# Retention scores of two heads in one step, and a new plan of who sums which modulation block

## What is computed

```python
mod = c_act @ w_ada[l] + b_ada[l]
shift, scale, gate = jnp.split(mod, 3, axis=-1)
h = _rmsnorm(x, norm_g[l]) * (1.0 + scale[:, None, :]) + shift[:, None, :]
z = h @ w_in[l]                      # 13 pieces of 512 columns
# Fourier mix, neighbourhood attention, retention, convolution, each times silu(gate piece)
y = jnp.concatenate([o_fft, o_na, o_ret, o_cv], axis=-1) @ w_out[l]
x = x + gate[:, None, :] * y
```

## Time and profile before

| | us |
|---|---|
| median of 3 runs | 2259.01 |
| lowest and highest of them | 2250.01, 2264.5 |
| the profiled execution | 2253.18 |
| its span | 2251.6 |
| TensorE busy in the span | 2164.1 (96%) |
| VectorE busy | 1480.2 (66%) |
| ScalarE busy | 962.4 (43%) |
| moved by DMA | 509.82 MB, mean 226 GB/s |

### The profile page before, as it was taken

The page is one execution under the profiler, slowest core; times in us unless marked ns, Lnnn a source line. Parts: engine busy times, 40 slices in busy tenths (PEclk is TensorE's granted clock), DMA queues, the critical chain, the costliest instruction groups (busy, mean ns, idle before and its releaser), DMA issues.

```text
span 2251.6 us, 33030 instructions
## 1 busy us (share of the span) xinstructions
PE 2164.1 (96%) x13686; PEld 1808.6 (80%) x13686; DVE 1480.2 (66%) x1904; ACT 962.4 (43%) x1337; POOL 201.7 (9%) x385
## 2 busy tenths in 40 slices
PE   5979999999899999999999999999999999999998
PEld 3768878887878878886888888787777989988876
DVE  0445879876655887765696756667776868445654
ACT  2324554554434554555632222223446444444443
POOL 2201111110011111100010100000100001000000
PEclk8989999999999999999999999999999999999999
DMA  9989886777598777676485646454875778422253
GB/s 367 401 265 311 275 319 234 273 269 275 153 315 299 258 265 250 226 269 235 157 294 162 219 131 196 152 184 147 284 256 174 238 249 280 136 67 65 88 188 131
DMA packets 225454, 509.82 MB, mean 226 GB/s; under 512 B 36065, under 2 KB 40289, under 8 KB 222753
## 3 DMA queue, kind: packets, MB, share of 16 engines
q1 hardware_dynamic: 170320, 300.49, 39.9%
q0 software_dynamic: 54304, 202.79, 26.3%
q10 hardware_dynamic: 688, 4.55, 0.5%
HBM read 499.38 MB, written 8.39 MB: 226 GB/s over the span
## 4 chain that ended last, share of the span: by engine, by line
PE 79%; DMA 8%; DVE 7%; ACT 2%; issue 2%; SPq 1%; POOL 0%; DVEq 0%; ACTq 0%; POOLq 0%
PE ps L768 23%; PE ps L769 22%; PE ps L770 22%; PE ps L824 3%; DMA w_raw<-in_w_in 3%; DMA ada_raw<-in_ada_w 2%; DVE ada_acc L2172 2%; PE ps L1439 1%; DVE wl L2252 1%; DMA rsw<-in_ada_w 1%; SPq L604 1%; DMA w_raw<-in_w_out 1%; PE ps L956 1%; PE ps L969 1%; PE ps L1165 1%
## 5 line engine op out<-in xcount | busy, mean ns | idle before, releaser
L2259 DVE TENSOR_TENSOR wl<-w_raw,wh 128x1024 fp32r<-128x1024 f32 x280 | 334.8, 1222 | 243.7 <-ACT wh L1543 242.6
L1543 ACT ACTIVATE wh<-w_raw 128x1024 fp32r<-128x1024 f32 x280 | 291.7, 1056 | 384.6 <-PE ps L770 253.6
L1596 ACT ACTIVATE wh<-w_raw 128x1024 fp32r<-128x1024 f32 x220 | 230.7, 1058 | 435.1 <-PE ps L770 391.0
L768 PE MATMUL ps<-hh,wh 128*128 128x256 f32 x1280 | 374.4, 292 | 11.2 <-DVE hl L2312 8.1
L2252 DVE TENSOR_TENSOR wl<-w_raw,wh 128x1024 fp32r<-128x1024 f32 x220 | 266.7, 1221 | 178.6 <-ACT wh L1596 178.4
L769 PE MATMUL ps<-hh,wl 128*128 128x256 f32 x1280 | 362.5, 283 | 0.0
L770 PE MATMUL ps<-hl,wh 128*128 128x256 f32 x1280 | 361.9, 283 | 0.0
L2172 DVE SCALAR_TENSOR_TENSOR ada_acc<-ada_raw,cpad,ada_acc 128x1024 f32<-128x1024 f32 x264 | 330.8, 1280 | 15.4 <-DMA ada_raw<-in_ada_w 13.2
L768 PEld LDWEIGHTS ps<-hh,wh 128*128 128x128 f32 x1280 | 244.2, 191 | 37.0 <-issue 21.5
L768 PE MATMUL ps<-wh,act_hl 128*128 128x512 f32 x640 | 256.6, 401 | 0.2 <-DVE wl L2252 0.2
L769 PE MATMUL ps<-wh,act_hl 128*128 128x512 f32 x640 | 253.3, 396 | 0.0
(11 more groups left out here) (374 smaller groups left out, 3346.1 us busy)
## 6 DMA issues: line engine op xcount, KB each, us to landing
ada_raw<-in_ada_w POOLq DMA_DIRECT2D x272, 512.0 KB, 5.1
w_raw<-in_w_in SPq DMA_DIRECT2D x208, 512.0 KB, 5.6
w_raw<-in_pool_in SPq DMA_DIRECT2D x72, 512.0 KB, 4.6
w_raw<-in_w_out SPq DMA_DIRECT2D x64, 512.0 KB, 5.6
w_raw<-in_mla_in SPq DMA_DIRECT2D x56, 512.0 KB, 4.6
ada_fourth<-in_ada_w POOLq DMA_DIRECT2D x48, 512.0 KB, 6.0
w_raw<-in_pool_out SPq DMA_DIRECT2D x48, 512.0 KB, 5.0
w_raw<-in_mla_out SPq DMA_DIRECT2D x32, 512.0 KB, 4.2
```

The source lines that it names most:

```text
L768: pe.matmul(dst, ah, bh, start=start, stop=False, skip_group_check=True)
L1543: act.activation(wh[:, g % RING, :], w_raw[:, g % RING, :], ACT.Copy).then_inc(w_hi, 1)
L1596: act.activation(wh[:, r, :], w_raw[:, r, :], ACT.Copy).then_inc(w_hi, 1)
L2259: dve.tensor_tensor(wl[:, g % RING, :], w_raw[:, g % RING, :], wh[:, g % RING, :].bitcast(F32), ALU.subtract).then_inc(w_lo, 1)
```

## The change

1. **Scores.** At every second step from 16 to 22, TensorE multiplies heads h and h + 1 together: four instructions, alternately on rows 0 to 63 and 64 to 127, head h into bank 4, head h + 1 into bank 5. It waits for `rt_p` of head h - 1, as before. VectorE reads bank `4 + h % 2`. Bank 5 is thus in use from step 16 to 23.
2. **Plan.** No modulation block is summed on TensorE in steps 17 to 24. Blocks by step (layer 0, VectorE + TensorE): steps 3 to 6 had 10 in all and now have 16, steps 8 to 11 had 14 and now have 11, step 18 had 2 + 0 and steps 19 to 24 had 2 + 2 each (now 1 + 0, at step 24 2 + 0), steps 27 to 31 had 1, 0, 2, 1, 1 and now have 4, 5, 3, 3, 3. Layer 1: steps 3 to 8 are as before; steps 10, 12 and 14 to 17 have one more each, on VectorE; steps 18 to 24 had 1 + 3, 1 + 3, then 1 + 2 (2 + 2 at 24) and now have 1, 1, 0, 0, 0, 0, 0; steps 25 to 32 had 0, 3, 3, 2, 2, 3, 3, 0 and now have 4, 4, 4, 4, 5, 1, 5, 5.
3. **The last piece is shared.** Of piece 5, VectorE sums the first 8 blocks in layer 0 and the first 10 in layer 1, TensorE the others; `ada_sum` then adds VectorE's part onto the same bank. In layer 1 this piece is for two conditioning vectors, so each of VectorE's 10 blocks takes two instructions, and the sum two vectors. In all TensorE sums 94 blocks where it summed 112, in 57 groups where there were 67 (counted from the tables by the rule of `ada_middle`); VectorE runs 28 instructions more; the sums over partitions are of 8 vectors, where they were of 5.
4. The first sum at step 24 waits for the last `rt_p` (which step 24 waits for in any case), piece 3 of layer 0 is summed in bank 6, and the context's first turn waits for `small_mul` instead of a read of bank 4.

```diff
--- before.py
+++ after.py
@@ -88,26 +88,51 @@
 TAP_ORDER = [CENTRE] + [i for i in range(TAPS) if i != CENTRE]
 
 
-def spread(j, t0, counts):
-
-    k, out = 0, {}
+def spread(j, t0, counts, k=0, end=ADA_SLOTS):
+
+    out = {}
     for t, n in enumerate(counts):
         out[t0 + t] = [(j, k + i) for i in range(n)]
         k += n
-    assert k == ADA_SLOTS
+    assert k == end
     return out
 
 
-ADA_DVE = [{**spread(0, 0, [1] * 8 + [2, 1, 2, 1, 2]), **spread(1, 13, [1, 2, 1] + [2] * 6),
-            **spread(3, 22, [2] * 5 + [1, 0, 2, 1, 1, 1])},
-           {**spread(0, 0, [1] * 2 + [2] * 5 + [1, 2, 1]), **spread(1, 10, [1] * 14 + [2])}]
-ADA_PE = [{**spread(2, 3, [1, 1, 2, 2, 2, 2, 3, 3]), **spread(4, 12, [4] + [3] * 4), **spread(5, 19, [2] * 8)},
-          {**spread(2, 2, [1, 2, 2, 2, 3, 3, 3]), **spread(3, 11, [3] * 4 + [2] * 2), **spread(4, 18, [3] * 2 + [2] * 5),
-           **spread(5, 26, [3, 3, 2, 2, 3, 3])}]
-ADA_FIN = [{11: 2, 17: 4, 18: 0, 27: 5, 28: 1, 34: 3}, {9: 2, 10: 0, 17: 3, 25: 4, 28: 1, 32: 5}]
-ADA_SUMMED = [(0, 1, 3), (0, 1)]
+def joined(*parts):
+
+    out = {}
+    for part in parts:
+        for t, slots in part.items():
+            out.setdefault(t, []).extend(slots)
+    return out
+
+
+ADA_SPLIT = [8, 10]
+ADA_DVE = [joined(spread(0, 0, [1, 1, 1, 2, 2, 2, 2, 1, 2, 1, 1]),
+                  spread(1, 11, [1, 2, 1, 2, 2, 2, 2, 1, 1, 1, 1]),
+                  spread(3, 22, [1, 1, 2, 2, 1, 1, 2, 2, 2, 2]),
+                  spread(5, 26, [1] * 8, 0, ADA_SPLIT[0])),
+           joined(spread(0, 0, [1] * 2 + [2] * 5 + [1, 2, 1]),
+                  spread(1, 10, [2, 1, 2, 1, 2, 2, 2, 2, 1, 1]),
+                  spread(5, 25, [1] * 6 + [2] * 2, 0, ADA_SPLIT[1]))]
+ADA_PE = [joined(spread(2, 3, [2, 2, 2, 2, 2, 3, 3]), spread(4, 12, [4] + [3] * 4),
+                 spread(5, 25, [2] * 4, ADA_SPLIT[0])),
+          joined(spread(2, 2, [1, 2, 2, 2, 3, 3, 3]), spread(3, 11, [3] * 4 + [2] * 2),
+                 spread(4, 25, [3, 3, 3, 3, 4]), spread(5, 31, [3, 3], ADA_SPLIT[1]))]
+ADA_FIN = [{10: 2, 11: 0, 17: 4, 24: 1, 32: 3, 34: 5}, {9: 2, 10: 0, 17: 3, 24: 1, 30: 4, 33: 5}]
+ADA_SUMMED = [(0, 1, 3, 5), (0, 1, 5)]
 ADA_BANKS = [7 if t <= 17 else 5 for t in range(STEPS)]
-ADA_FIN_BANKS = [ADA_BANKS, [4 if t == 28 else b for t, b in enumerate(ADA_BANKS)]]
+ADA_FIN_BANKS = [[6 if t == 32 else b for t, b in enumerate(ADA_BANKS)], ADA_BANKS]
+
+
+def ada_vectors(l, j):
+
+    return ((0, 1), (1, 2)) if l + (j > 1) == DEPTH else ((ADA_SUMMED[l].index(j) % 2, 0),)
+
+
+def ada_begins(l, j):
+
+    return ADA_SPLIT[l] if j == 5 else 0
 ADA_AHEAD = range(8, SMALL_STEP)
 CTX_SSQ, CTX_VAR = OUT_STEP + 2, OUT_STEP + 4
 CTX_TURN = {(5, 0): 0, (5, 1): 1, (5, 3): 2, (6, 0): 3, (6, 2): 4, (6, 3): 5, (7, 1): 6, (7, 2): 7}
@@ -214,7 +239,7 @@
 
 ADA_MORE, DVE_AFTER = ada_more_schedule()
 PE_SUM = {16: 1, 17: 2, 18: 3, 19: 4, 20: 5, 21: 6 + ADA_SLOTS - LAST_DVE}
-ADA_PE_LAYERS = max(x[5] for x in ADA_SEQ if x[4])
+ADA_PE_LAYERS = max(ADA_DONE.values())
 
 
 def both_vectors(n):
@@ -826,13 +851,14 @@
                                    skip_group_check=True)
                 mm.then_inc(ada_pe, 1)
 
-            def ada_sum(v, row_, bank_):
+            def ada_sum(v, row_, bank_, start=True, more=False):
 
                 for q in range(4):
                     mm = pe.matmul(ps[32 * q:32 * q + 32, bank_, 0:256], opad[:, 32 - row_:64 - row_],
-                                   ada_acc[:, v, q * 256:(q + 1) * 256], start=True, stop=True,
+                                   ada_acc[:, v, q * 256:(q + 1) * 256], start=start, stop=not more,
                                    tile_position=(0, 32 * q), skip_group_check=True)
-                mm.then_inc(ada_pe, 1)
+                if not more:
+                    mm.then_inc(ada_pe, 1)
 
             def ada_turn(event, bank_):
 
@@ -945,18 +971,20 @@
                         pe.matmul(ps[:, 6, SEQ:2 * SEQ], tb("head_mean"), sq_t, start=True, stop=True
                                   ).then_inc(rt_ssq, 1)
                     h = t - RET0
-                    if 0 <= h < HEADS:
+                    if 0 <= h < HEADS and h % 2 == 0:
                         if h == 0:
                             pe.wait_ge(piece_fin, l * NFIN + 3)
                         else:
                             pe.wait_ge(rt_p, l * HEADS + h)
-                        lo = 64 * (h % 2)
                         q_, k_ = chunks(rq), chunks(rk)
                         for j in range(TT):
-                            mm = pe.matmul(ps[:, 4, j * SEQ:(j + 1) * SEQ],
-                                           k_[lo:lo + 64, h // 2, j * P:(j + 1) * P],
-                                           q_[lo:lo + 64, h // 2, :], start=True, stop=True)
-                        mm.then_inc(rt_scores, 1)
+                            for head in (h, h + 1):
+                                lo = 64 * (head % 2)
+                                mm = pe.matmul(ps[:, 4 + head % 2, j * SEQ:(j + 1) * SEQ],
+                                               k_[lo:lo + 64, h // 2, j * P:(j + 1) * P],
+                                               q_[lo:lo + 64, h // 2, :], start=True, stop=True)
+                                if j == TT - 1:
+                                    mm.then_inc(rt_scores, 1)
                     g = (t - FFT0) // 2
                     if 0 <= g < NCH and (t - FFT0) % 2 == 0:
                         if g == 0:
@@ -994,9 +1022,13 @@
                         j = ADA_FIN[l][t]
                         pe.wait_ge(ada_used, max(x[5] for x in ADA_SEQ if not x[4] and x[:3:2] == (l, j)) + ADA_RING)
                         pe.wait_ge(ada_read, ada_event(l, t))
-                        if ADA_FIN_BANKS[l][t] == 4:
-                            pe.wait_ge(small_mul, l * 4 + 4)
-                        ada_sum(ADA_SUMMED[l].index(j) % 2, 0, ADA_FIN_BANKS[l][t])
+                        if t == LN0:
+                            pe.wait_ge(rt_p, l * HEADS + HEADS)
+                        if ADA_FIN_BANKS[l][t] == 6:
+                            pe.wait_ge(rt_var, l * 4 + 4)
+                        vecs = ada_vectors(l, j)
+                        for v, row_ in vecs:
+                            ada_sum(v, row_, ADA_FIN_BANKS[l][t], j != 5, (v, row_) != vecs[-1])
 
                 def ada_middle(t, i):
 
@@ -1009,10 +1041,10 @@
                             seen += 1
                             if i != (2 if here < 3 else 1 if seen < 3 and t not in ADA_FIN[l] else 3):
                                 continue
-                            if k == 0:
+                            if k == ada_begins(l, j):
                                 pe.wait_ge(ada_read, max([4 + 6 * l] + [ada_event(l, x) + 1 for x in ADA_FIN[l] if x < t]))
                             pe.wait_ge(*ada_here(q))
-                            ada_slot(ada_buf(q % ADA_RING_A), k, ADA_BANKS[t])
+                            ada_slot(ada_buf(q % ADA_RING_A), k, ADA_BANKS[t], ada_begins(l, j))
 
                 for t in range(2 * NP_):
                     ada_first(t)
@@ -1064,7 +1096,7 @@
 
                     if n == 0:
                         pe.wait_ge(b_xn, 1)
-                        pe.wait_ge(ada_read, ada_event(1, 28) + 1)
+                        pe.wait_ge(small_mul, 4 + 4)
                     if n >= 2:
                         pe.wait_ge(b_ht, n - 1)
                     for kk in range(2):
@@ -2458,7 +2490,7 @@
                         dve.wait_ge(rt_dec, l * HEADS + h + 1)
                         if h >= 2:
                             dve.wait_ge(rt_pv, l * HEADS + h - 1)
-                        dve.tensor_tensor(rp[:, h % 2, :], ps[:, 4, :], dec[:, :], ALU.mult).then_inc(rt_p, 1)
+                        dve.tensor_tensor(rp[:, h % 2, :], ps[:, 4 + h % 2, :], dec[:, :], ALU.mult).then_inc(rt_p, 1)
                     h = t - RET0 - 2
                     if 0 <= h < HEADS and h % 2:
                         dve.wait_ge(rt_std, l * 4 + h // 2 + 1)
@@ -2485,8 +2517,7 @@
                         if not by_pe and (layer, step) == (l, t):
                             if k:
                                 dve.wait_ge(ada_used, n - 1 + ADA_RING)
-                            v = ADA_SUMMED[l].index(j) % 2
-                            ada_slot(ada_buf(q % ADA_RING_A), *ada_here(q), k, k == 0, ((v, 0),))
+                            ada_slot(ada_buf(q % ADA_RING_A), *ada_here(q), k, k == 0, ada_vectors(l, j))
 
                 def ada_done(t):
 
```

## The result

| | before | after |
|---|---|---|
| median (lowest to highest) of 11 runs each, us | 2256.86 (2249.51 to 2264.5) | 2267.92 (2265.03 to 2279.49) |
| span of the profiled execution | 2251.6 | 2265.4 |
| TensorE busy | 2164.1 | 2157.9 |
| rest of the span | 87.5 | 107.5 |
| mean granted TensorE clock | 0.986 | 0.978 |

A forecast was written before the change was run, and what follows sets the result against it. It took TensorE, busy 2164 of 2252 us, as the bound. Terms -17.0 + 0.5 + 3.5 + 4 + 3 + 1 = -5.0 us took the median from 2259 to 2254 us, range 2239 to 2269.

The forecast's parts named there:

- TensorE's stream, -17.0: Both layers: fewer blocks and groups save 10.1 us, paired scores 8.7, more sums cost 1.8; 17.0 us shorter.
- Check (1): Retention scores: L956's successor has the same 64 records, and two heads take 1.15 us.
- (2): TensorE's blocks: L824's successor has 144 records fewer, and none between steps 17 and 24.
- (3): Layer 0's steps 19 to 23 are about 1.1 and 2.2 us shorter in turn; if less, VectorE sets them.
- VectorE, +0.5: Layer 1's step 19: VectorE keeps its block while TensorE loses three; 0.5 us taken, at worst 2.6.
- rival C: Layer 1's steps 25 to 32: VectorE becomes the bound; +8.6 us, 2268 us; chance 0.12.
- Step 31, +3.5 through the variance chain: Layer 1: VectorE's two blocks delay variance, ScalarE's root and step 32's weights; TensorE stands 3.5 us, bounds 0 and 5.1.
- Check (6): Layer 1: the first slot of step 32 waits about 3.5 us for `wl`.
- a block is 512 KB whoever sums it; what changes is when: All block transfers: size and number stay the same whichever engine sums them; only their timing changes.
- Transfers, +8 (4, 3, 1): Added stalls at transfer bursts: 4 us in layer 0's steps 3 to 6, 3 in 27 and 28, 1 in layer 1's 27 to 29.
- (4): Layer 0's steps 3 to 6 together are 4 us longer plus the price of two blocks; otherwise the transfers fit.
- (5): Layer 0's steps 27 to 29 show waits for blocks or `wl`.

The follow-up runs named there:

- e14: Kernel before, with three quarters of each later block's transfer left out and TensorE's blocks first in the buffers: 2236.21 us.
- e13: Changed kernel, with three quarters of each later block's transfer left out and TensorE's blocks first in the buffers: 2214.14 us.
- e5: Changed kernel with the context's variance made ahead of VectorE's two blocks in layer 1's step 31: 2270.92 us, ratio 1.0069.
- e2: Changed kernel with TensorE's blocks first in the buffers in steps 0 to 7 and 26 on: 2250.52 us, ratio 0.9967.
- quarter cut: Three quarters of each later block's transfer left out, in the kernel before (2234.08 us) and in the changed one (2224.44 us).

## Why the prediction was wrong

**TensorE's stream, -17.0: right.** Blocks, scores and sums were counted well. With both causes away (e14, e13) TensorE is busy 2160.3 us in the kernel before and 2142.3 in the changed one, 18.0 less. Check (1) held (64 records, 1.16 us a pair; 8.3 of 8.7 us measured by the medians, 9.9 by the windows), (2) as well (L849 has 784 records on `ada_raw` and `ada_fourth` where L824 had 928, and none in steps 17 to 24), and (3) (1.19 and 2.45 us in turn; only step 23 is shorter by 0.6 alone, and it is not VectorE that sets it, with 14.9 us of work in its 16.6: the new sum of piece 1 (L857, at 440.87) goes ahead of step 24's first slot and so falls into this window).

**VectorE, +0.5, and rival C: nothing to be seen.** Layer 1's step 19 is 1.95 us shorter, of 1.75 priced. Of the 0.5 us taken for VectorE no run shows anything. Rival C gave 2268, and the median is 2267.92, but by another mechanism: the version with TensorE's blocks first has all 28 instructions of VectorE and is 17.4 us faster. A time that fits a rival is no evidence for it; its own check was the wait for `wl` in several of the last steps, and that is shorter than before.

**Step 31, +3.5 through the variance chain: wrong, and this is the step that failed.** The step did get longer, by 7.7 us where 3.5 was taken, but the variance has no part in these 7.7: made early (e5), it takes nothing off. I found VectorE's two new blocks in this step and followed one thing that is queued behind them, the small pair and ScalarE's root. I did not follow the other: the buffer that the first of them frees, the GpSimd instruction that waits for it, and the transfers behind that. Check (6) failed: `wl` is not waited for at step 32; TensorE is late before that, at its third block of step 31. The root's lateness is real (ScalarE waits for it until 1071.59) and hidden behind TensorE's stand. Where the stand is gone (e2), step 31 is 1.0 us longer than before, and there the forecast chain does show, with 0.2 us of waiting for `bm`, which follows the root, and 0.3 for `wl`: 0.5 us, not 3.5.

The same omission hides in "a block is 512 KB whoever sums it; what changes is when". It also changes who frees the buffer, and when in the step. No term of the sum held it: it was put at nothing. Undoing it in the changed kernel is worth 17.4 us with full transfers, and 10.3 with light ones. That the time moved the other way than forecast is this omission, together with the transfers below. That 2267.92 still lies between 2239 and 2269 is luck: those bounds were made of other terms.

**Transfers, +8 (4, 3, 1): right places, too small.** Here each stall is measured by how much the quarter cut takes away, more from the changed kernel than from the one before: layer 0's steps 3, 5 and 6 15.4 against 7.6, so 7.8 where 4 was taken (bounds 0 to 8.4); step 28 6.0 against 0 (3 was taken, 0 to 6.5); layer 1's steps 28 to 30 10.5 against 6.4, so 4.1 where 1 was taken (0 to 4). Together 17.9, and each near its upper bound. Two things make this soft. Steps 3, 5 and 6 took 58.3 to 64.3 us in the five executions that share their code (61.7 here), so the 7.8 could be 4 to 10. And the cut also shortens waits that the order makes: with TensorE's blocks first in all four kernels the same three differences are 5.7, 4.8 and 1.8, together 12, still more than 8. I had worked out 6 us too much for steps 27 and 28 and halved it for buffers that take transfers earlier or later, and they took little of it: by their windows 4.9 + 7.3 = 12.2 of the 12.7 MB went through there, in 31.6 us. Checks (4) and (5) thus held in kind: steps 3 to 6 are 10.9 us longer, not 4 plus two blocks, and step 28 waits 3.4 us for `ada_fourth`.

**The clock: a term that was not there.** Of the 18.0 us that TensorE's stream lost only 6.2 show in its busy time; the other 11.8 were given back as slower instructions. Where: the same changed instructions keep TensorE busy 15.6 us longer with both causes there than with both away, and 14.6 of these are in six steps whose clock is 0.73 to 0.91 (layer 0's 3, 6 and 28, layer 1's 28, 29 and 31); in the kernel before the same difference is 3.7. With 20.0 us more of not being busy the difference of the spans is -18.0 + 11.8 + 20.0 = +13.8; as the 11.8 is what was left over, this sum tests nothing. I had priced each stall by its length alone, though the earlier trace rows had clocks of 0.84 and 1.00 beside each other.

So, by the medians of the table, the change with both causes away is worth -22.1 us; the order then adds 12.5 and the bytes 20.7, or, taken the other way round, the bytes 17.7 and the order 15.5, to +11.1 in either case. I had -17, +8 and a chain of 3.5. How the bursts and the order share what only the two together cost was not taken apart.

## What to carry to other kernels

When several engines take blocks from one set of buffers that an in-order queue refills, write down for each buffer who frees it and at which point of that engine's step, and follow the queue behind it, before bytes are counted: a change of who uses a block is a change of when every later block arrives. Put the blocks in the buffers in the order in which they are really used, counting each engine's place in the step. And price a stall of TensorE with what the clock takes behind it (here 2.3 us on top of 5.4), and, when the queues around it are already full, a burst above the middle of its range: here they came to 12 to 18 us together where I took 8.

## What the hardware showed that I had not expected

- Behind a stand of 5.4 us the clock was at half (0.50 from 1074 to 1078), and 2.3 of the stall's 7.7 us came after it had ended.
- One core moved 402 GB/s through the 14.9 us of the changed kernel's layer 1 step 27, more than the 391 of the earlier trace rows. The Trainium skill ("HBM Reference", Specifications (TRN2)) says that a core streaming alone measures well above the per-core share; that agrees, and the 358 of the page cited in the prediction is no limit here.
- The same 512 KB block lands 4.2 us after its issue in a quiet step and 15.6 us after it beside two transfers of 2 MB. The lead that this plan's four buffers give was not enough for the second: TensorE stood 6.8 and 0.9 us for the blocks of that step.
